# Block products for the conv output projection of a hybrid encoder kernel on eight Trainium2 cores

## The reference

```python
y_conv = c_b * short_conv_centred(c_c * c_x, conv_w) * jax.nn.silu(c_z)
p_conv = jnp.einsum('blc,cd->bld', y_conv, w_out_c)
...
y_gla = o * jax.nn.silu(r)
p_gla = jnp.einsum('blc,cd->bld', y_gla, w_out_g)
merged = jax.nn.sigmoid(m_a) * p_conv + jax.nn.sigmoid(m_b) * p_gla
out = jnp.einsum('bld,de->ble', merged, w_out)
return h + rms_norm(out, g_post)
```

## Time and profile before

| | |
|---|---|
| median of three runs | 2921.14 us (lowest 2919.9) |
| the profiled execution | 2921.19 us, span of its slowest core 2919.6 us |
| the eight cores' spans | 2909.6 to 2919.6 us |
| granted TensorE clock | 0.995 to 0.997 |
| busy: PE, DVE, ACT, POOL | 98%, 62%, 47%, 28% |

### The profile page before, as it was taken

How to read it: one execution, slowest core, us unless ns; L and a number is a source line. 1 busy time by engine, 2 the same in 40 slices (tenths; PEclk the granted TensorE clock), 3 DMA queues, 4 the chain that set the end, 5 groups by cost and what they waited for, 6 DMA issues and landing times.

```text
span 2919.6 us, 53947 instructions; the slowest of 8 cores (2909.6 to 2919.6 us)
## 1 busy us (share of the span) xinstructions
PE 2851.8 (98%) x16092; PEld 1468.0 (50%) x16092; DVE 1815.4 (62%) x2786; ACT 1381.3 (47%) x2567; POOL 831.7 (28%) x1278
## 2 busy tenths in 40 slices
PE   6999999999999999999999999999999999999998
PEld 3565644444456554444456555444445655544443
DVE  4766662564677776465476677556457777745554
ACT  5766651232456764232256686323235767522222
POOL 3343333331323223232242312223123222321212
PEclk9999999999999999999999999999999999999999
DMA  7786548853633334374373323447356322354334
GB/s 183 134 140 116 125 101 183 232 173 113 197 106 77 75 84 115 110 232 127 111 216 81 75 68 89 123 142 230 97 152 170 78 72 71 84 137 127 118 112 140
DMA packets 340764, 373.44 MB, mean 128 GB/s; under 512 B 208112, under 2 KB 218352, under 8 KB 339968
## 3 DMA queue, kind: packets, MB, share of 16 engines
q1 hardware_dynamic: 326944, 344.61, 41.8%
q0 software_dynamic: 13536, 25.37, 6.0%
HBM read 287.69 MB, written 63.50 MB: 120 GB/s over the span
## 4 chain that ended last, share of the span: by engine, by line
PE 94%; DMA 2%; DVE 1%; issue 1%; POOL 1%; ACT 0%; SPq 0%; DVEq 0%; POOLq 0%; ACTq 0%
PE ps L479 94%; DMA sb_onT<-x 0%; DMA sb_onT<-sb_ON 0%; DMA wsc<-sb_W 0%; DMA sb_W<-w_all 0%; DMA sb_KT<-sb_GR 0%; POOL sb_stat L674 0%; PE ps L484 0%; POOL sb_SB L514 0%; DMA sb_ycT<-x 0%; DVE sb_CS L509 0%; DVE sb_ycT L505 0%; DVE sb_TB L509 0%; POOL sb_stat L514 0%; DVE sb_CS L505 0%
## 5 line engine op out<-in xcount | busy, mean ns | idle before, releaser
L479 PE MATMUL ps<-sb_uT,sb_W 128*128 128x512 bf16 (+2 forms) x7840 | 1625.9, 366 | 1.9 <-DMA sb_W<-w_all 1.2
L479 PEld LDWEIGHTS ps<-sb_uT,sb_W 128*128 128x128 bf16 (+1 forms) x7840 | 707.8, 98 | 808.9 <-issue 20.4
L496 ACT ACTIVATE sb_CS<-ps 128x512 f32<-128x512 f32 (+2 forms) x528 | 281.2, 540 | 636.2 <-PE ps L479 605.2
L505 DVE TENSOR_TENSOR sb_CS<-ps,sb_CS 128x512 f32<-128x512 f32 (+1 forms) x408 | 281.0, 691 | 187.9 <-PE ps L479 177.6
L509 DVE SCALAR_TENSOR_TENSOR sb_CS<-sb_CS,ps 128x512 f32<-128x512 f32 x256 | 175.8, 687 | 295.6 <-PE ps L479 284.3
L505 POOL TENSOR_TENSOR sb_GR<-sb_CS 128x512 bf16<-128x512 f32 x128 | 162.1, 1267 | 671.0 <-DVE sb_CS L509 658.5
L479 PE MATMUL ps<-sb_GR 128*128 128x512 bf16 (+2 forms) x1792 | 347.5, 318 | 1.1 <-POOL sb_GR L505 1.1
L505 POOL TENSOR_TENSOR sb_CS<-sb_CS 128x512 f32<-128x512 f32 x128 | 164.8, 1291 | 276.7 <-DVE sb_CS L509 168.6
L479 PE MATMUL ps<-sb_V,sb_uT 128*128 128x256 bf16 x2048 | 239.3, 274 | 0.0
L479 PE MATMUL ps<-sb_onT,sb_W 128*128 128x512 bf16 x1024 | 232.2, 379 | 2.6 <-DVE sb_onT L509 2.6
L509 DVE SCALAR_TENSOR_TENSOR sb_CS<-sb_CS,sb_convw 128x512 f32<-128x512 bf16 x256 | 209.8, 832 | 39.8 <-ACT sb_CS L496 27.6
(11 more groups left out here) (125 smaller groups left out, 2888.7 us busy)
## 6 DMA issues: line engine op xcount, KB each, us to landing
sb_W<-wsc SPq DMA_DIRECT2D x440, 256.0 KB, 2.6
sb_onT<-x SPq DMA_DIRECT2D x56, 512.0 KB, 5.4
sb_W<-wst SPq DMA_DIRECT2D x112, 256.0 KB, 2.8
sb_W<-w_all POOLq DMA_DIRECT2D x80, 256.0 KB, 6.2
sb_GR<-x SPq DMA_DIRECT2D x40, 512.0 KB, 5.5
wsc<-sb_W SPq DMA_DIRECT2D x80, 256.0 KB, 4.4
y<-sb_GR SPq DMA_DIRECT2D x32, 512.0 KB, 3.4
sb_ycT<-x SPq DMA_DIRECT2D x32, 512.0 KB, 5.4
```

The source lines that it names most:

```text
L479: S.add("pe", lambda e: e.matmul(out, lhsT=lhsT, rhs=rhs, start=start, stop=stop, skip_group_check=more), r, w, cost=max(0.025, free_n(rhs ...
L496: S.add("act", lambda e: e.activation(out=out, in_=in_, func=func, **kw), r, w, table=TABLE.get(func), cost=0.17 + 0.82e-3 * free_n(in_) + ...
L505: S.add(eng, lambda e: e.tensor_tensor(out=out, in0=a, in1=b, op=op), r, w, cost=ecost(eng, free_n(out), narrow(out, a, b)))
```

## The change

Outside the plain stage the conv projection is computed by `Seven` too, over a pair of feature blocks d and d+1 by the two token groups, so that it needs 28 matmuls of 512 columns for 32. For this the sums of weights of four pairs (8 to 11 in `wst`) are made in the plain stage, and `ysums` makes four block sums of ycT (`TY`, in the upper part of GR) in each other stage. The merge stage now goes in pairs: a pair has three sets p1 to p7 (gates of d, gates of d+1, conv of d and d+1) with the four og products laid between p7 and p4 and at the end; the token groups of og run as s=1, s=0. `finy` does the (tanh + 1) times the product: for p2 straight from PSUM, for p3, p7 and p4 an addition into the side sum and a multiply-add of two SBUF tiles. The gates have two sets of buffers (CS, and G2 of 8 KB), GpSimd's sums have a chain of their own (`MG`). W1 has five buffers. The last stage 7 has four buffers each for x and the result; all its additions are on VectorE. The space for GpSimd's DMA descriptors is set to 4096. Loads of x for stage 7 wait for the stage's last oc, and a tile is put in order only when the sums it reads are.

```diff
-    nc = bass.Bass("TRN2", target_bir_lowering=False)
+    nc = bass.Bass("TRN2", target_bir_lowering=False, dynamic_dma_scratch_size=4096)
...
-    wst_d = nc.dram_tensor("wst", [8 * 128 * 8, 256], BF16, kind="Internal").ap()
+    wst_d = nc.dram_tensor("wst", [12 * 128 * 8, 256], BF16, kind="Internal").ap()
...
-                       ("AT", 12 * KB), ("CS", 16 * KB), ("W1", 3 * 2048), ("W2", 5 * 2048), ("V", 4 * KB),
+                       ("AT", 12 * KB), ("CS", 16 * KB), ("W1", 5 * 2048), ("W2", 5 * 2048), ("V", 4 * KB),
                        ("TF", 2 * KB), ("TB", 2 * KB), ("SB", 5 * 512), ("KT", 2 * KB), ("SM", KB), ("ON", 3 * KB),
-                       ("MT", 1280)]:
+                       ("MT", 1280), ("G2", 8 * KB)]:
...
-        w1 = WPool("W1", [Buf("W1", i * 2048, 2048) for i in range(3)])
+        w1 = WPool("W1", [Buf("W1", i * 2048, 2048) for i in range(5)])
...
-        ta = [Buf("CS", z * 2048, 2048) for z in range(2)]
-        tb2 = [Buf("CS", 4096 + z * 2048, 2048) for z in range(2)]
+        ta = [Buf(r, z * 2048, 2048) for r in ("CS", "G2") for z in range(2)]
+        tb2 = [Buf(r, 4096 + z * 2048, 2048) for r in ("CS", "G2") for z in range(2)]
         sd1, sd2, sd5 = (Buf("CS", 8192 + z * 2048, 2048) for z in range(3))
         TT = [Buf("AT", 0, 4096), Buf("AT", 4096, 4096), Buf("AT", 8192, 4096), Buf("V", 0, 4096)]
+        TY = [Buf("GR", 32 * KB + i * 4096, 4096) for i in range(4)]
...
-                            slot_free = [("t7", b - 1, 1, 7)] if half or s else [("st", b - 1, 0, 7)]
+                            slot_free = [("t7", b - 1, 1, 7)] if half or s else [("oc", b - 1, 1, 7, 1)]
...
+        def ysums(b, hh, gates_):
+
+            for bf in range(4):
+                for part in range(2 if bf in (0, 2) and hh else 1):
+                    put("TT", lambda bf=bf, part=part: ysum(hh, bf, part), ("TY", b, hh, bf, part), gates_)
+
+        def yv(hh, j, n, t):
+
+            if hh == 1 and j < 2:
+                ap, keys = REG["ycX"][:, :], [g for z in range(j, j + n) for g in ycT(1, z)(BF16, t, 512)[1]]
+            else:
+                ap, keys = REG["ycT"][:, :], [g for z in range(j, j + n) for g in Buf("ycT", z * 2048, 2048)(BF16, t, 512)[1]]
+            return ap.rearrange("p (k t) -> p k t", t=1024)[:, j:j + n, t:t + 512], keys
+
+        def ysum(hh, bf, part):
+
+            j, n = (0, 4) if bf in (1, 3) or not hh else (2 * part, 2)
+
+            def tv(i):
+                ap, keys = TY[i](BF16, j * 512, n * 512)
+                return ap.rearrange("p (k t) -> p k t", t=512), keys
+
+            x = {0: lambda: yv(hh, j, n, 512), 1: lambda: yv(hh, 4, 4, 512), 2: lambda: yv(hh, 4 + j, n, 512), 3: lambda: yv(hh, 4, 4, 0)}[bf]()
+            y = {0: lambda: yv(hh, j, n, 0), 1: lambda: tv(0), 2: lambda: yv(hh, j, n, 512), 3: lambda: tv(1)}[bf]()
+            o = tv(bf)
+            tt("dve", o[0], x[0], y[0], ALU.subtract, x[1] + y[1], o[1])
...
+            def finy(d, f, s, bk, s_=None):
+                a_ap, a_k = ta[f * 2 + s](F32)
+                if s_ is None:
+                    stt(a_ap, a_ap, 1.0, bk[0][:, 0:512], ALU.add, ALU.mult, bk[1] + a_k, a_k)
+                    return
+                s_ap, s_k = s_(F32)
+                tt("dve", s_ap, bk[0][:, 0:512], s_ap, ALU.add, bk[1] + s_k, s_k)
+                stt(a_ap, a_ap, 1.0, s_ap, ALU.add, ALU.mult, s_k + a_k, a_k)
...
-                a_ap, a_k = (ta if n == "oc" else tb2)[s](F32)
+                a_ap, a_k = (ta if n == "oc" else tb2)[d % 2 * 2 + s](F32)
                 stt(a_ap, a_ap, 1.0, bank[:, 0:512], ALU.add, ALU.mult, bk + a_k, a_k)
-                if n == "og":
-                    t_ap, t_k = ta[s](F32)
-                    m_ap, m_k = mT[d](BF16, s * 512, 512)
-                    tt("pool", m_ap, t_ap, a_ap, ALU.add, t_k + a_k, m_k)
-                if s == 1:
+                if last and n == "oc":
+                    if d % 2:
+                        sums_w(G[("ho", d - 1)], h, 8 + d // 2)
+                        rel(G[("ho", d - 1)])
+                        rel(h)
+                    else:
+                        G["ho", d] = h
+                elif last:
                     rel(h)
+
+            def merge(d, s):
+                t_ap, t_k = ta[d % 2 * 2 + s](F32)
+                a_ap, a_k = tb2[d % 2 * 2 + s](F32)
+                m_ap, m_k = mT[d](BF16, s * 512, 512)
+                tt("pool", m_ap, t_ap, a_ap, ALU.add, t_k + a_k, m_k)
...
+            sets = (("p1", None), ("p5", 0), ("p6", 1), ("p2", None), ("p3", None), ("p7", 2), ("p4", 3))
+            for d in range(0, 8, 2):
                 units = {}
-                if plain:
-                    hm = {n: w2.reserve((n, d)) for n in ("ma", "mb")}
-                    for n in ("ma", "mb"):
-                        for s in range(2):
-                            units[n, s] = (lambda n=n, s=s, d=d, hm=hm: gate(hm[n], d, s, n, hm["ma"]), (n, b, hh, d, s), [])
-                else:
-                    sv = Seven((b, hh, d), d, ("ma", d), ("mb", d), t0, fin)
-                    for p, fn, ti in (("p1", sv.p1, None), ("p5", sv.p5, 0), ("p6", sv.p6, 1), ("p2", sv.p2, None), ("p3", sv.p3, None),
-                                      ("p7", sv.p7, 2), ("p4", sv.p4, 3)):
-                        units[p] = (fn, ("mb", b, hh, d, 1) if p == "p4" else ("sv", b, hh, d, p),
-                                    [("TT", b, hh, ti)] if ti is not None else [])
-                ho = {n: w1.reserve((n, d)) for n in ("oc", "og")}
-                for n in ("oc", "og"):
+                ho = [w1.reserve(("og", d))]
+                for z in range(2):
+                    sv = Seven(d + z, ("ma", d + z), ("mb", d + z), uu, TT, lambda f, s, bk, s_=None, z=z: fin(d + z, f, s, bk, s_), w2)
+                    sv.last()
+                    for p, ti in sets:
+                        units[z, p] = (unit_of(sv, p), ("mb", b, hh, d + z, 1) if p == "p4" else ("sv", b, hh, d + z, p),
+                                       [("TT", b, hh, ti)] if ti is not None else
+                                       [("mt", b, hh, d - 2 + z, s) for s in range(2)] if p == "p2" and d else [])
+                sv = Seven(8 + d // 2, ("oc", d), ("oc", d + 1), yy, TY, lambda f, s, bk, s_=None: finy(d, f, s, bk, s_), w1)
+                ho.append(w1.reserve(("og", d + 1)))
+                sv.last()
+                nm = {"p2": (d, 0), "p3": (d, 1), "p7": (d + 1, 0), "p4": (d + 1, 1)}
+                for p, ti in sets:
+                    units[2, p] = (unit_of(sv, p), ("oc", b, hh) + nm[p] if p in nm else None,
+                                   [("TY", b, hh, ti, int(hh and ti in (0, 2)))] if ti is not None else [])
+                for z in range(2):
                     for s in range(2):
-                        units[n, s] = (lambda n=n, s=s, d=d, ho=ho: outp(ho[n], d, s, n, ysrc if n == "oc" else osrc),
-                                       (n, b, hh, d, s), [("rm", b, 7, 0)] if n == "og" else [])
-                if plain:
-                    order = [("ma", 0), ("ma", 1), ("oc", 0), ("oc", 1), ("mb", 0), ("mb", 1), ("og", 0), ("og", 1)]
-                else:
-                    order = ["p1", "p5", "p6", "p2", "p3", "p7", ("oc", 0), "p4", ("oc", 1), ("og", 0), ("og", 1)]
-                for o in order:
-                    if d == 0 and o == ("og", 0):
+                        units["og", z, s] = (lambda s=s, d=d, z=z, ho=ho: outp(ho[z], d + z, s, "og", osrc, s == 0),
+                                             ("og", b, hh, d + z, 1 - s), [("rm", b, 7, 0)])
+                six = ["p1", "p5", "p6", "p2", "p3", "p7"]
+                for o in ([(0, p) for p in six] + [("og", 0, 1), (0, "p4")] + [(1, p) for p in six] + [("og", 0, 0), (1, "p4")] +
+                          [(2, p) for p in six] + [("og", 1, 1), (2, "p4"), ("og", 1, 0)]):
+                    if d == 0 and o == ("og", 0, 1):
                         for it in late:
                             put("D2", *it)
                     put("D2", *units[o])
+                for z in range(2):
+                    for s in ((0, 1), (1, 0))[z]:
+                        put("MG", lambda d=d, z=z, s=s: merge(d + z, s), ("mt", b, hh, d + z, s),
+                            [("og", b, hh, d + z, 1 - s), ("oc", b, hh, d + z, s if z == 0 else 1 - s)])
...
             def add(il):
-                yv, yk = yout[hh][il % 2](F32)
-                xv, xk = xres[hh][il % 2](F32)
-                eng = min(("pool", "dve"), key=lambda e: max(S.free[e], S.free["pe"]) + ecost(e, 1024, False))
-                tt(eng, yv, yv, xv, ALU.add, yk + xk, yk)
+                yv, yk = ybuf(il)(F32)
+                xv, xk = xbuf(il)(F32)
+                tt("dve", yv, yv, xv, ALU.add, yk + xk, yk)
...
-                tiles.append((lambda il=il: tile(il), ("t7",) + me, []))
+                tiles.append((lambda il=il: tile(il), ("t7",) + me, [("mt", b, hh, d, il // 4) for d in range(8)]))
```

(2 more changed lines are left out.)

73 lines of the change are left out of this document (52 added, 21 removed).

## The result

The changed kernel takes 2949.2 us (two runs: 2949.17 and 2949.32), against 2919.9 and 2921.1 of the kernel before: a ratio of 1.0098, 95% interval 1.0055 to 1.0142. The forecast was 2919.6 in a range of 2902 to 2934, so the kernel came out some 30 us slower than forecast (and 28 us slower than the kernel before), outside the range.

A forecast was written before the change was run, and what follows sets the result against it. The prediction took TensorE's list of matmuls, busy 98% of the span, as the bound. From 2921.2 us its terms (-24.2 + 8.2 + 5.6 + 8.0 + 2.0 - 1.2 = -1.6) gave 2919.6 us, range 2902 to 2934.

The forecast's parts named there:

- term 1: Conv projection in seven merge stages: 112 matmuls fewer at 0.216 us each, -24.2 us.
- the rule of 131 ns: Skill page's spacing for 512-column matmuls, by which term 1 would be 14.7 us; rival of 2929 us, chance 0.02.
- Term 3: Third set: VectorE's two-input multiply-adds held up by GpSimd's sums make p4 wait 0.2 us in 28 pairs, +5.6 us.
- Term 4: First tile behind a stage's last product waits for GpSimd's sum, four times 2.0 us, +8.0 us.
- Term 2: Entry of half 0, batches 1 to 3: onT waits sum to 10.0, less 1.8 gained before p4, net +8.2 us.
- At nothing: VectorE in the merge stages: extra additions and block sums fit in its idle half, priced at zero, 0.69 each otherwise.
- Batch 0: First merge stage: transposes have 3.5 us less to hide behind, five buffers end some waits; +2, bounds -4 and +8.
- slower through batch 0: Rival: SP's order of weight-sum stores and transposes costs landings in two or three blocks, +12 to +18, 2935 us; chance 0.12.
- The tail: End of the kernel: GpSimd drops the last-but-one addition, the last is shorter, a multiplication skips a store wait; -1.2 us.

The follow-up runs named there:

- e13: e10 with direct conv products in the seven later merge stages and no block sums of ycT: ratio 1.0000 to the kernel before, mean span +0.8.
- e10: e8 with the wo load issued later and W1 loads for batch 0's second merge stage held behind tile 5 of the first: ratio 0.9957.
- e3: Changed kernel with the sums of the gated products made by VectorE, not GpSimd, outside the first merge stage: ratio 1.0173 to the kernel before.
- e15: e10 with p3's multiply-add put behind p7's addition and one GpSimd sum ordered later: 2897.4 us (one run), mean span -20.5.
- e2: Changed kernel with the second block's attention products run as tokens 0 up, then 512 up: ratio 1.0064 to the kernel before.
- e4: Changed kernel with direct conv products in the seven later merge stages and no block sums of ycT: ratio 1.0098 to the kernel before.
- e7: Changed kernel with e2's order, half 0's first attention products behind the second set, and block sums laid singly behind p7 and p4: ratio 1.0005.
- e11: Changed kernel with the 2 MB load of wo issued only behind p4 of the second block: ratio 1.0069 to the kernel before.
- e5: Kernel before with five W1 buffers for three and descriptor space of 4096: ratio 1.0022 to the unedited kernel before.
- e8: e7 with W1 loads held to three of the five buffers until the first merge stage: 2923.4 and 2927.1 us, mean span -0.5.

## Why the prediction was wrong

**Right.** The bound, and term 1: e13 against e10, and the unchanged distance of 216 ns, bear out the price of a matmul; the rule of 131 ns is not seen. Term 3: 6.5 us for 5.6; e3 shows the stretched durations and e15 that the place of the multiply-add makes p4 late, while the step between them, 0.23 us each, rests on the rows. Term 4 at tile 0: 1.8, 1.8, 1.8 and 1.9 us for 4 x 2.0; e2 shows the cover to be its cause, and e4, where nothing piles up, has the 1.07 that the term took as 1.0. Term 2 by size: 7.0 us for 10.0, with 1.6 gained at p4 for 1.8.

**The step that failed** is "At nothing: [...] the block sums [...] fit in its idle half". The stage has the room, 50.8 of 104 us before. But VectorE goes through its list in order, and the scheduler put the sums, as soon as they could run, ahead of additions that TensorE needs at once. The price I gave ("0.69 each on the path if not") was asked of the average and never of the place: the order list of the changed kernel showed the three sums ahead of the additions of p5 and p6. It cost 9.6 us at the half-1 entries (10.2 from start to start), part of the onT waits, and the half clock behind them. Laid one by one behind p7 and p4 the same sums no longer cost the 9.6 us (e7).

**The step that was missing** is the clock. Every wait was priced at its length. At seven to ten places a core (the start of the program left out) the clock fell behind a wait and cost 1.2 to 2.9 us again, 10.8 us more in all than before. It was to be seen in the trace before: core 7 has 17 matmuls at half clock at 405 us, 2.7 us, behind waits of 2.2 and 2.5.

**Mis-sized terms.** Batch 0 was +10.6 for +2. The forecast's reason, transposes behind SyncE's other issues, was right, and e11 names the issue (the 2 MB load). But it priced the shift by 16 matmuls only and gave the five W1 buffers as a gain; e5 shows them (with the descriptor space) as about half of the loss, since they change the order from the start. The load near 567 us, 5.8, was in no term. The rival *slower through batch 0* named this place and 12 to 18 us, near what it took with its half clock; it was given 0.12, and alone would not have reached 2949. The tiles had 4.5 us more than term 4, from 0.78 twice at the first tiles of half 1 in batches 0 to 2, of which I had said that 40 matmuls of cover suffice; e2's order ends most of these too. The tail gained 4.9 for 1.2, and the forecast's reason for it, the last additions, is not the main one: e5, which leaves them as they were, already gains 3.8 (13.3 to 9.5). Which part of e5's edit does that is not shown.

**A right size by half of the cause.** Term 2 put the onT waits of batches 1 to 3 down to the landing of the transposes alone, rising from 1.5 to 4.8 over the batches. They were 2.3, 2.9 and 2.5 (core 6), ended by VectorE, whose four block sums (put at nothing) stood ahead of its multiplications. The landing was a real bound, but the lower of two: without the load 7.1 of 8.4 remain (e11), without the block sums 6.2 (e4). The attention product simply comes before VectorE's four multiplications, and e7, which lays it later, ends the wait.

**Left open.** Why the order of batch 0 with five buffers loses is told only by its waits: e8 mends one and makes another. The load near 567 us (5.8) has no run of its own. Whether term 3's wait is the stretching of the multiply-add or more of its place was not separated.

## What to carry to other kernels

Price an added operation at its place in its engine's list: what stands right behind it, and who waits for that. An idle half of an engine hides nothing that stands ahead of the operation that frees a PSUM bank, and the remedy is to lay small pieces in the gaps, since the same sums cost 9.6 us at the half-1 entries in a block and nearly nothing there spread. Where TensorE is the bound, add to each new wait of more than two us what the clock takes behind it (here 1.2 to 2.9 us). Where two things bound the same wait, removing one of them gains only the distance to the other. And when a resource of a list scheduler is made larger, compare the order of the whole program, since parts that the change never touched may be laid anew.

## What was not expected of the hardware

The half clock behind waits, 1.2 to 2.9 us at a place, and that it differs between cores that run the same program: 11.6 to 16.5 us a core in one execution. Over all the traces of this case (the cores whose matmul records are complete, waits that stand alone), none of 424 waits of 1.0 to 1.95 us was followed by matmuls at half clock, 3 of 15 between 1.95 and 2.3, 157 of 201 between 2.3 and 2.75, 46 of 70 between 2.75 and 4, and all 82 longer ones. A DMA transpose of sb_ON that SyncE issues behind a 2 MB load landed some 10 us after its issue, and in e11, without the load ahead, 2.4 to 3.3 us after it. VectorE's two-input multiply-adds of 128x512 take 0.69 us alone, and up to 1.32 beside a GpSimd sum of 1.27.
